# Expert weights fetched as 2 MB of one expert in 16 KB pieces instead of 2 MB of two experts in 8 KB pieces

## The chip, the core and the metric

One core of a Trainium2 chip runs the whole program. The metric is the device time of one execution in microseconds (us); lower is better. TensorE (PE in the profile) multiplies matrices, VectorE (DVE) and ScalarE (ACT) work on tiles, GpSimd (POOL) does little here, SyncE (SP) issues the loads, and 16 DMA engines carry them.

## What is computed

Two layers of a small transformer, float32 throughout, for 256 tokens of width 2048. Each layer is a mixer (layer 0: mLSTM and gated linear attention; layer 1: sparse attention), a layer norm, a mixture of 16 experts, and a layer norm. The change touches the mixture only:

```
# each token picks 2 of 16 experts (comb holds the two gates, 0 elsewhere)
hg = einsum('btd,edf->btef', x, w_gate)      # w_gate[e]: 2048 x 512
hu = einsum('btd,edf->btef', x, w_up)        # w_up[e]:   2048 x 512
h  = silu(hg) * hu * comb
y  = einsum('btef,efd->btd', h, w_down)      # w_down[e]: 512 x 2048
```

All three matrices of all 16 experts of both layers, 403 MB, are read from memory once. Of each, a partition holds 32 KB in one run (`gate_w`, `up_w`, `down_w` are arranged so).

## The kernel before

**Experts in pairs.** The experts of a layer are done two at a time, eight pairs `x` = 0 to 7. Up to 64 tokens (CAP) of each expert are gathered; matmuls of the two experts alternate (`for e in range(2)`), each with 64 columns of weights, writing to halves of the same PSUM bank. Four pairs make a group: in a group's first pair (`i == 0`) TensorE also gathers the tokens of its eight experts (`gather_tile`, 16 tiles of 4 matmuls, lines 841 and 842; DVE line 1626 and ACT line 1187 copy them out of two banks). So pairs 0 and 4 of each layer carry a gather.

**Steps.** The weights of a pair come in 12 steps of 2 MB: steps 0 to 3 are gate, 4 to 7 up, 8 to 11 down. I number a layer's steps through, 0 to 95; pair 4 begins with step 48. There are six slots of 2 MB (`step_slot`: three in `arena2`, three in `ring`); step n lands in slot n modulo 6. SP issues load n (`load_step`, line 485) once `step_used` says that step n - 6 has been used. The six first loads of a layer are issued ahead, during the mixer's end. TensorE waits for `loaded`, does the step's 8 matmuls (16 instructions in the profile, since each float32 matmul is run as two), and adds one to `step_used`.

**Between steps.** In the second and later pairs TensorE adds the last pair's result to the tokens (`add_elder`, `scatter`, lines 850 and 851) after steps 1 and 3, and twice around the transposes (line 899) ahead of step 8. Where tokens are gathered, four tiles come ahead of each of the steps 0 to 3, and each of these steps also waits until the tiles have been copied out (`drained`).

**After the experts.** The loads of the second layer norm's rows and, from layer 0, of the next mixer's weights (line 471, into the ring's slots as steps 9 to 11 are used, and line 507) stand behind the expert loads in SP's order. The mixer's weights come in 2 KB pieces. When the last step is used, ACT and DVE read the result out (lines 1197 and 1630), TensorE scatters it (line 850), and the layer norm follows.

Of the kernel before, what the change touches and what calls it, by code (L numbers as in the profile page):

```python
# [18 lines left out]
BANK = 512  # L19
SLOT = 4096  # L20
# [9 lines left out]
CAP = 64  # L30
# [5 lines left out]
HALF = SLOT // 2  # L36
# [46 lines left out]
def program(nc, a, out):  # L83
    first, drained_by, n = {}, "", 0
# [7 lines left out]
    with ctx:  # L92
# [133 lines left out]
        hT_e, o = carve(arena, o, [4, P])  # L226
# [6 lines left out]
        def xc(k):  # L233

            return xc_lo[:, k, :] if k < KT // 2 else xc_hi[:, k - KT // 2, :]

        aff, k = carve(arena, xc_at, [TT, NE])
        sel, k = carve(arena, k, [TT, NE])
        rank, k = carve(arena, k, [TT, NE])
        cmp, k = carve(arena, k, [TT, NE])  # L240
        cmp2, k = carve(arena, k, [TT, NE])
        pairs6, k = carve(arena, k, [TT * NG, 6])
        gsc, k = carve(arena, k, [TT, NG])
        grank, k = carve(arena, k, [TT, NG])
        gcmp, k = carve(arena, k, [TT, NG])
        gcmp2, k = carve(arena, k, [TT, NG])
        chosen, k = carve(arena, k, [TT, NE])
        csum, k = carve(arena, k, [TT, 1])
        crec, k = carve(arena, k, [TT, 1])
        logits_T, k = carve(arena, k, [SEQ])  # L250
# [21 lines left out]
        w_small1, k = carve(arena2, o, [KT, 80])  # L272
        R, o2 = carve(arena2, o, [IH, SEQ])
        rope_t, k = carve(arena2, o, [4, TT * (IH + 1) * IDH // 8])

        X, k = [[None, None], [None, None]], o
# [6 lines left out]
        rope_q, k = carve(arena2, k, [4, TT * GQ * 16])  # L283

        ps = [ctx.enter_context(nc.psum_tensor(f"ps{i}", [P, BANK], FP32)) for i in range(8)]
# [11 lines left out]
        drained = {"A": sem("drained_by_act"), "D": sem("drained_by_dve")}  # L297
# [53 lines left out]
        for lay in range(2):  # L351
            s = {name: sem(f"{name}_{lay}") for name in (
                "step_used", "silu_ready", "pT_full", "pT_ready", "h_ready", "hT_full", "hT_ready",
                "y_hi_ready", "y_ready", "comb_ready", "pick_ready", "h_hi_ready", "h_lo_ready", "acc_ready")}
# [56 lines left out]
        gate_w = a["moe_w_gate"].rearrange("l e (p k) n -> l e p (k n)", k=KT)  # L411
        up_w = a["moe_w_up"].rearrange("l e (p k) n -> l e p (k n)", k=KT)
        down_w = a["moe_w_down"].rearrange("l e (p j) n -> l e p (j n)", j=4)


        def step_slot(st):

            b = st % 6
            return arena2[:, b * SLOT:(b + 1) * SLOT] if b < 3 else ring[:, (b - 3) * SLOT:(b - 2) * SLOT]

        def group_tiles(g):


            return 0 if isinstance(g, int) and g == 0 else 24 * g - 4

        def gather_at(first, n):


            return n if first or n < 4 else n + 1
# [10 lines left out]
        def _(sp):  # L440
# [33 lines left out]

            def step_source(lay, e, st):

                w = (gate_w, up_w, down_w)[st // 4]
                two = w[lay, e:e + 2] if isinstance(e, int) else w[lay, bass.ds(e, 2)]
                return two.rearrange("e p f -> p e f")[:, :, (st % 4) * HALF:(st % 4 + 1) * HALF]

            def load_step(lay, e, x, st):

                if not (isinstance(x, int) and x == 0 and st < 6):
                    sp.wait_ge(M[lay]["step_used"], STEPS * x + st - 5)
                sp.dma_start(step_slot(st).rearrange("p (e f) -> p e f", e=2), step_source(lay, e, st))\
                  .then_inc(M[lay]["loaded"][st % 6], 16)

            def wait_last_pair(st):
# [117 lines left out]
        def _(pe):  # L606
# [121 lines left out]
            for k in range(KT):  # L728
                for at, lo, hi in ((0, 0, NH), (32, NH, 2 * NH), (64, 8, 8 + RANK)):
                    last = nc.tensor.matmul(tile("gates")[at:at + hi - lo, 0:SEQ], w_small0[:, k, lo:hi], hT[:, k, :],  # L730
                                            start=(k == 0), stop=(k == KT - 1), skip_group_check=True)
# [5 lines left out]
            for i in range(2):  # L737
                drained_before(pe, "decay", i)
                for j in range(2):
                    hd = 2 * i + j  # L740
                    last = nc.tensor.matmul(tile("decay", i)[:, j * SEQ:(j + 1) * SEQ], w2[0:RANK, hd * DK:(hd + 1) * DK],
                                            t3[0:RANK, 0:SEQ], start=True, stop=True)
# [24 lines left out]
            for c in range(3):  # L767
                for hp in range(2):
                    i = 2 * c + hp
                    drained_before(pe, "gstate", i)  # L770
                    for j in range(2):
                        hd = 2 * hp + j
                        last = nc.tensor.matmul(tile("gstate", i)[:, j * DV:(j + 1) * DV], kz[:, (c // 2) * NH + hd, c % 2, :],
                                                V[:, c // 2, NH + hd, 0:DV], start=True, stop=True)
# [9 lines left out]
            for tt in range(TT):  # L784
                pe.wait_ge(state_ready, 6 if tt else 2)
                for hp in range(2):
                    i = 2 * tt + hp
# [19 lines left out]
            def experts(lay):  # L807

                s = M[lay]
# [41 lines left out]
                        nc.tensor.matmul(t, to, y_lo[:, c % 2, :], start=False, stop=True).then_inc(s["full"][tt], 1)  # L851

                def project(x, i, m, bank):
                    st = 4 * bank + m
                    pe.wait_ge(s["loaded"][st % 6], 16 * (2 * x + st // 6 + 1))
                    w = step_slot(st).rearrange("p (e k n) -> p e k n", e=2, k=4)
                    for kk in range(4):
                        k = 4 * m + kk
                        for e in range(2):
                            at = (2 * i + e) * CAP  # L860
                            last = nc.tensor.matmul(ps[bank][e * CAP:(e + 1) * CAP, :], xc(k)[:, at:at + CAP], w[:, e, kk, :],  # L861
                                                    start=(k == 0), stop=(k == KT - 1), skip_group_check=True)
                    last.then_inc(s["step_used"], 1)

                def pair(g, i, first):
                    x = GPAIRS * g + i

                    def add_elder(c):
                        if not (first and i == 0):
                            scatter(x - 1, (i + 1) % 2, c, group_tiles(g) + scatter_at(first, i, c))  # L870

                    for m in range(4):
                        if i == 0:
                            for k in range(4 * m, 4 * m + 4):
                                gather_tile(g, first, k)
                            for b in range(2):
                                pe.wait_ge(s["drained"][b], group_tiles(g) + gather_at(first, 2 * m + 1) + 1)
                        project(x, i, m, 0)
                        if m % 2 == 1:
                            add_elder(m // 2)  # L880
                    project(x, i, 0, 1)
                    project(x, i, 1, 1)

                    pe.wait_ge(s["silu_ready"], x + 1)
                    mine = slice(i * P, (i + 1) * P)
                    for tt in range(TT):
                        nc.tensor.transpose(ps[0][:, tt * P:(tt + 1) * P], pick8[:, tt, mine].bitcast(FP32), ident[:, :])
                    for tt in range(TT):
                        last = nc.tensor.matmul(ps[0][:, SEQ:SEQ + 2], pick8[:, tt, mine].bitcast(FP32), comb_g[:, tt, 2 * i:2 * i + 2],
                                                start=(tt == 0), stop=(tt == TT - 1), skip_group_check=True)  # L890
                    last.then_inc(s["pT_full"], 1)
                    project(x, i, 2, 1)
                    project(x, i, 3, 1)
                    add_elder(2)

                    pe.wait_ge(s["pT_ready"], x + 1)
                    pe.wait_ge(s["h_ready"], x + 1)
                    for j in range(4):
                        last = nc.tensor.transpose(ps[0][:, j * P:(j + 1) * P], h_e[:, j::4], ident[:, :])
                    last.then_inc(s["hT_full"], 1)  # L900
                    add_elder(3)
                    pe.wait_ge(s["hT_ready"], x + 1)
                    if not (first and i == 0):
                        pe.wait_ge(s["y_ready"], 4 * x)
                    for j in range(4):
                        st = 8 + j
                        pe.wait_ge(s["loaded"][st % 6], 16 * (2 * x + 2))
                        w = step_slot(st).rearrange("p (e n) -> p e n", e=2)
                        for c in range(4):
                            for e in range(2):  # L910
                                last = nc.tensor.matmul(ps[2 + c][e * CAP:(e + 1) * CAP, :], hT_e[:, j, e * CAP:(e + 1) * CAP],  # L911
                                                        w[:, e, c * BANK:(c + 1) * BANK], start=(j == 0), stop=(j == 3), skip_group_check=True)
                        last.then_inc(s["step_used"], 1)

                def group(g, first):
                    pe.wait_ge(s["pick_ready"], g + 1)
# [962 lines left out]
```

## Time and profile before

| what | value |
|---|---|
| median of 3 runs | 1990.96 us (1990.54 to 1991.87) |
| the profiled execution, its own time | 1990.97 us |
| its span, first to last instruction | 1988.8 us |
| TensorE busy | 1743.0 us, 88% of the span |
| DVE, ACT busy | 506.9 us, 286.9 us |
| DMA read | 532.67 MB, 269 GB/s over the span |
| expert stretches (about 585 to 1011 us and 1531 to 1957 us) | 421 GB/s |

A busy share is an average over stages with different limits. A row of the timeline gives the start of a group of instructions, how long it took, the engine, the line of the kernel, what it writes and reads, and in brackets how long the engine sat idle before it and what ended that. SPq is SP's queue: its rows are the moments at which loads are issued.

### The profile page before, as it was taken

What the parts mean: (1) busy time and instruction counts of PE and PEld (TensorE: products, weight loads), DVE (VectorE), ACT (ScalarE), POOL (GpSimd) and SP (SyncE); (2) the same over time, 40 slices, a digit from 0 to 9 for tenths busy, and PEclk for the clock granted to TensorE, in tenths of its full rate; (3) what the DMA queues carried; (4) which work ended last, traced back from release to release, by engine and by line L of the source; (5) the groups of instructions that cost most, each with busy time, mean ns of one, the idle gap of its engine ahead of it and who ended that gap; (6) DMA issues with size and microseconds to landing.
All of it is one profiled execution on the core that took longest, in us unless ns stands there. A gap on an engine that the chain in (4) does not pass through costs nothing.

```text
span 1988.8 us, 16588 instructions
## 1 busy us (share of the span) xinstructions
PE 1743.0 (88%) x6849; PEld 869.6 (44%) x6849; DVE 506.9 (25%) x955; ACT 286.9 (14%) x453; POOL 17.7 (1%) x36
## 2 busy tenths in 40 slices
PE   7999999999599888998769999978959978899874
PEld 5884444477343223332234454436834322343221
DVE  1201011445611112111160171324461111211115
ACT  1012011332310001100010001223331000110000
POOL 1000000000000000000000000000000000000000
PEclk9999999999699999999979999989979999999997
DMA  6443433282379999999972433327337999999995
GB/s 226 142 169 127 169 127 127 86 331 90 127 313 421 421 422 421 421 422 421 421 301 85 138 116 127 127 85 268 112 127 302 421 421 421 422 421 421 421 421 214
DMA packets 121327, 535.82 MB, mean 269 GB/s; under 512 B 12916, under 2 KB 12952, under 8 KB 70568
## 3 DMA queue, kind: packets, MB, share of 16 engines
q1 hardware_dynamic: 120680, 530.59, 67.2%
q0 software_dynamic: 576, 4.19, 0.5%
q8 instruction: 55, 0.90, 0.2%
q14 instruction: 16, 0.13, 0.0%
HBM read 532.67 MB, written 2.10 MB: 269 GB/s over the span
## 4 chain that ended last, share of the span: by engine, by line
PE 53%; issue 28%; DMA 13%; DVE 4%; ACT 1%; SPq 1%; POOL 0%; DVEq 0%; POOLq 0%
PE ps L662 22%; DMA ring<-in_moe_w_down 8%; PE ps L861 6%; PE ps L644 6%; DMA ring<-in_moe_w_up 5%; PE ps L686 3%; PE ps L685 3%; PE ps L684 3%; PE ps L911 3%; PE ps L614 1%; PE ps L841 1%; PE ps L1005 1%; PE ps L842 1%; PE ps L970 1%; PE ps L939 0%
## 5 line engine op out<-in xcount | busy, mean ns | idle before, releaser
L662 PE MATMUL ps<-ring,hT 128*128 128x512 f32 x1024 | 441.7, 592 | 0.0
L662 PEld LDWEIGHTS ps<-ring,hT 128*128 128x128 f32 x1024 | 194.0, 190 | 239.9 <-issue 239.6
L911 PE MATMUL ps<-ring,arena 128*64 128x512 f32 x768 | 173.4, 597 | 31.7 <-DMA ring<-in_moe_w_down 31.7
L861 PE MATMUL ps<-arena 128*64 128x512 f32 x768 | 174.5, 598 | 23.6 <-DMA arena<-in_moe_w_up 18.5
L861 PE MATMUL ps<-arena,hT 128*64 128x512 f32 x512 | 115.8, 597 | 28.2 <-DMA arena<-in_moe_w_gate 21.2
L1636 DVE TENSOR_TENSOR arena<-ps,arena 128x512 f32<-128x512 f32 x128 | 82.3, 684 | 203.4 <-PE ps L851 203.4
L861 PE MATMUL ps<-ring,hT 128*64 128x512 f32 x512 | 115.1, 596 | 12.1 <-DMA ring<-in_moe_w_up 12.1
L911 PEld LDWEIGHTS ps<-ring,arena 128*64 128x64 f32 x768 | 51.9, 137 | 151.5 <-issue 89.1
L644 PE MATMUL ps<-hT,ring 128*128 128x256 f32 x512 | 110.8, 379 | 0.0
L1630 DVE TENSOR_TENSOR y_lo<-ps,y_hi 128x512 fp32r<-128x512 f32 x64 | 42.4, 683 | 264.4 <-ACT y_hi L1197 264.4
L861 PEld LDWEIGHTS ps<-arena 128*64 128x64 f32 x768 | 52.0, 136 | 125.4 <-issue 90.2
L684 PE MATMUL ps<-w_lo,x_hi 128*128 128x512 f32 x256 | 101.7, 397 | 4.7 <-DVE x_lo L1839 3.0
L644 PEld LDWEIGHTS ps<-hT,ring 128*128 128x128 f32 x512 | 97.2, 190 | 13.6 <-issue 0.4
L686 PE MATMUL ps<-w_hi,x_lo 128*128 128x512 f32 x256 | 102.2, 399 | 0.0
L685 PE MATMUL ps<-w_hi,x_hi 128*128 128x512 f32 x256 | 101.9, 398 | 0.0
L1489 DVE TENSOR_TENSOR w_lo<-ring,w_hi 128x2048 fp32r<-128x2048 f32 x32 | 73.3, 2293 | 92.9 <-ACT w_hi L1049 92.9
L1197 ACT ACTIVATE y_hi<-ps 128x512 fp32r<-128x512 f32 x64 | 36.5, 596 | 403.1 <-PE ps L911 268.5
L861 PEld LDWEIGHTS ps<-arena,hT 128*64 128x64 f32 x512 | 35.9, 137 | 103.9 <-issue 68.6
L1049 ACT ACTIVATE w_hi<-ring 128x2048 fp32r<-128x2048 f32 x32 | 61.4, 1925 | 109.4 <-PE ps L686 109.4
L861 PEld LDWEIGHTS ps<-ring,hT 128*64 128x64 f32 x512 | 35.8, 137 | 84.5 <-issue 61.5
L861 PE MATMUL ps<-ring,arena 128*64 128x512 f32 x256 | 58.3, 597 | 13.9 <-DMA ring<-in_moe_w_gate 10.6
L850 PE MATMUL ps<-y_hi,pick_T 128*128 128x512 f32 x128 | 59.7, 467 | 10.2 <-DVE arena L1636 7.2
(278 smaller groups left out, 1373.7 us busy)
## 6 DMA issues: line engine op xcount, KB each, us to landing
arena<-in_moe_w_gate SPq DMA_DIRECT2D x48, 2048.0 KB, 24.6
ring<-in_moe_w_down SPq DMA_DIRECT2D x48, 2048.0 KB, 25.8
ring<-in_moe_w_up SPq DMA_DIRECT2D x32, 2048.0 KB, 26.1
arena<-in_moe_w_up SPq DMA_DIRECT2D x32, 2048.0 KB, 24.2
ring<-in_ab_w_in SPq DMA_DIRECT2D x24, 2048.0 KB, 7.9
ring<-in_moe_w_gate SPq DMA_DIRECT2D x16, 2048.0 KB, 25.9
arena<-in_moe_w_down SPq DMA_DIRECT2D x16, 2048.0 KB, 24.1
ring<-in_c_w_in SPq DMA_DIRECT2D x16, 2048.0 KB, 8.2
```

Source lines behind the costliest of these rows:

```text
L644: last = nc.tensor.matmul(tile(stage, j)[:, 0:SEQ], w[:, k, j * P:(j + 1) * P], hT[:, 8 * u + k, :], start=(u + k == 0), stop=(u == 1 and ...
L662: last = nc.tensor.matmul(tile(stage, i)[:, :], hT[:, 8 * u + k, tt * P:(tt + 1) * P], w[:, k, :], start=(u + k == 0), stop=(u == 1 and k ...
L684: nc.tensor.matmul(t, x_h, w_l[:, k, :], start=(part + k == 0), stop=False)
L685: nc.tensor.matmul(t, x_h, w_h[:, k, :], start=False, stop=False)
L686: last = nc.tensor.matmul(t, x_l, w_h[:, k, :], start=False, stop=(part + k == 6))
L850: nc.tensor.matmul(t, to, y_hi[:, c % 2, :], start=True, stop=False)
L861: last = nc.tensor.matmul(ps[bank][e * CAP:(e + 1) * CAP, :], xc(k)[:, at:at + CAP], w[:, e, kk, :], start=(k == 0), stop=(k == KT - 1), s ...
L911: last = nc.tensor.matmul(ps[2 + c][e * CAP:(e + 1) * CAP, :], hT_e[:, j, e * CAP:(e + 1) * CAP], w[:, e, c * BANK:(c + 1) * BANK], start= ...
L1049: act.activation(w_hi[:, q % 2, :], w, ACT.Copy).then_inc(w_hi_ready, 1)
L1489: v.tensor_tensor(lo, w, w_hi[:, q % 2, :].bitcast(FP32), ALU.subtract).then_inc(w_lo_ready, 1)
L1630: v.tensor_tensor(y_lo[:, c % 2, :], ps[2 + c][:, :], y_hi[:, c % 2, :].bitcast(FP32), ALU.subtract).then_inc(s["y_ready"], 1)
L1636: v.tensor_tensor(d, ps[6 + tt][:, :], d, ALU.add).then_inc(s["drained"][tt], 1)
```

## The change

A step is still 2 MB, in the same slot. What lies in it is different: before, it held a quarter of a matrix of both experts (8 KB a partition of each, so two pieces of 8 KB); now, it holds half of a matrix of one expert (one piece of 16 KB a partition). Even steps hold the first expert, odd steps the second. Since each pair of matmuls needs both experts, TensorE now waits for two steps at once, does 16 matmuls on them, and adds two to `step_used` at the end. The order of the matmuls is the same. The gather of tokens moves with it: eight tiles ahead of steps 0 and 1, eight ahead of steps 2 and 3. The scatters and transposes stay where they were in the order.

```
 def step_source(lay, e, st):
-    w = (gate_w, up_w, down_w)[st // 4]
-    two = w[lay, e:e + 2] if isinstance(e, int) else w[lay, bass.ds(e, 2)]
-    return two.rearrange("e p f -> p e f")[:, :, (st % 4) * HALF:(st % 4 + 1) * HALF]
+    w, half, mine = (gate_w, up_w, down_w)[st // 4], st % 4 // 2, st % 2
+    one = w[lay, e + mine] if isinstance(e, int) else w[lay, bass.ds(e + mine, 1)].rearrange("e p f -> (e p) f")
+    return one[:, half * SLOT:(half + 1) * SLOT]
...
-    sp.dma_start(step_slot(st).rearrange("p (e f) -> p e f", e=2), step_source(lay, e, st))\
+    sp.dma_start(step_slot(st), step_source(lay, e, st))\
...
 def project(x, i, m, bank):
-    st = 4 * bank + m
-    pe.wait_ge(s["loaded"][st % 6], 16 * (2 * x + st // 6 + 1))
-    w = step_slot(st).rearrange("p (e k n) -> p e k n", e=2, k=4)
-    for kk in range(4):
-        k = 4 * m + kk
+    st = 4 * bank + 2 * m
+    w = []
+    for e in range(2):
+        pe.wait_ge(s["loaded"][(st + e) % 6], 16 * (2 * x + st // 6 + 1))
+        w.append(step_slot(st + e).rearrange("p (k n) -> p k n", k=8))
+    for kk in range(8):
+        k = 8 * m + kk
         for e in range(2):
...
-    last.then_inc(s["step_used"], 1)
+    last.then_inc(s["step_used"], 2)
...
-    for m in range(4):
+    for m in range(2):
         if i == 0:
-            for k in range(4 * m, 4 * m + 4):
+            for k in range(8 * m, 8 * m + 8):
                 gather_tile(g, first, k)
             for b in range(2):
-                pe.wait_ge(s["drained"][b], group_tiles(g) + gather_at(first, 2 * m + 1) + 1)
+                pe.wait_ge(s["drained"][b], group_tiles(g) + gather_at(first, 4 * m + 3) + 1)
         project(x, i, m, 0)
-        if m % 2 == 1:
-            add_elder(m // 2)
+        add_elder(m)
...
-    for j in range(4):
-        st = 8 + j
-        pe.wait_ge(s["loaded"][st % 6], 16 * (2 * x + 2))
+    for m in range(2):
+        st = 8 + 2 * m
+        w = []
+        for e in range(2):
+            pe.wait_ge(s["loaded"][(st + e) % 6], 16 * (2 * x + 2))
+            w.append(step_slot(st + e).rearrange("p (j n) -> p j n", j=2))
+        for j in range(2 * m, 2 * m + 2):
...
-        last.then_inc(s["step_used"], 1)
+        last.then_inc(s["step_used"], 2)
```

On TensorE, the first use of weights in layer 0, before. Lines 841 and 842 are the gather, line 861 the projection; the names in brackets are the semaphores waited for.

```order
L841 MATMUL ps<-pick,h_hi 128x512
L842 MATMUL ps<-pick,h_lo 128x512
L861 MATMUL ps<-arena,hT 64x512 [waits expert_step_loaded_0_0,tile_drained_0_1,tile_drained_0_0]
L861 MATMUL ps<-arena,hT 64x512 x7
L841 MATMUL ps<-pick,h_hi 128x512 [waits tile_drained_0_0]
L842 MATMUL ps<-pick,h_lo 128x512
L841 MATMUL ps<-pick,h_hi 128x512
L842 MATMUL ps<-pick,h_lo 128x512
```

The same place of the changed kernel, where the projection is line 863.

```order
L841 MATMUL ps<-pick,h_hi 128x512
L842 MATMUL ps<-pick,h_lo 128x512
L863 MATMUL ps<-arena,hT 64x512 [waits expert_step_loaded_0_0,expert_step_loaded_0_1,tile_drained_0_1,tile_drained_0_0]
L863 MATMUL ps<-arena,hT 64x512 x15
L841 MATMUL ps<-pick,h_hi 128x512 [waits tile_drained_0_0]
L842 MATMUL ps<-pick,h_lo 128x512
L841 MATMUL ps<-pick,h_hi 128x512
L842 MATMUL ps<-pick,h_lo 128x512
```

Four more gather tiles stand ahead of it, the wait names two loads, and 16 matmuls follow in one run; the wait for copied tiles comes twice in such a pair of experts instead of four times.

The end of a pair of experts on TensorE, before: steps 10 and 11 (line 911), then steps 0 and 1 of the next pair.

```order
L911 MATMUL ps<-ring,arena 64x512 [waits expert_step_loaded_0_4]
L911 MATMUL ps<-ring,arena 64x512 x7
L911 MATMUL ps<-ring,arena 64x512 [waits expert_step_loaded_0_5]
L911 MATMUL ps<-ring,arena 64x512 x7
L861 MATMUL ps<-arena,hT 64x512 [waits expert_step_loaded_0_0]
L861 MATMUL ps<-arena,hT 64x512 x7
L861 MATMUL ps<-arena,hT 64x512 [waits expert_step_loaded_0_1]
L861 MATMUL ps<-arena,hT 64x512 x7
```

The same place of the changed kernel, the tail of steps 8 and 9 first.

```order
L913 MATMUL ps<-arena 64x512
L913 MATMUL ps<-ring,arena 64x512
L913 MATMUL ps<-ring,arena 64x512 [waits expert_step_loaded_0_5,expert_step_loaded_0_4]
L913 MATMUL ps<-ring,arena 64x512 x15
L863 MATMUL ps<-arena,hT 64x512 [waits expert_step_loaded_0_1,expert_step_loaded_0_0]
L863 MATMUL ps<-arena,hT 64x512 x15
```

Each step's 8 matmuls waited for their own load; now 16 wait for two.

## Rows read from the trace of the kernel before

**Rows 1.** The page: the span, and the DMA engines' share by slice in tenths.

```profile
span 1988.8 us, 16588 instructions
...
DMA  6443433282379999999972433327337999999995
```

**Rows 2.** Windows: busy time of each engine, granted clock, DMA share, GB/s.

```profile
656.00:716.00 60.00, 49.45 (x218) 16.59 (x218) 8.93 (x16) 4.23 (x9) 0.00 (x0) 1.00 1.01 421
1603.00:1663.00 60.00, 49.73 (x222) 16.71 (x220) 8.83 (x16) 3.86 (x7) 0.00 (x0) 1.00 1.01 421
582.40:584.90 2.50, 2.50 (x14) 0.86 (x12) 0.00 (x0) 0.00 (x0) 0.00 (x0) 1.00 1.02 429
1201.00:1204.00 3.00, 3.00 (x9) 1.33 (x8) 0.00 (x0) 0.00 (x0) 0.00 (x0) 1.00 1.05 410
```

**Rows 3.** Timeline of TensorE, pair 2 of layer 0, steps 8 to 11.

```profile
697.84 3.65 PE L911 MATMUL ps<-arena 128*64 128x512 f32 x16
701.41 3.65 PE L911 MATMUL ps<-ring,arena 128*64 128x512 f32 x16
706.38 3.65 PE L911 MATMUL ps<-ring,arena 128*64 128x512 f32 x16 [1.31 <-DMA ring<-in_moe_w_down]
711.35 3.65 PE L911 MATMUL ps<-ring,arena 128*64 128x512 f32 x16 [1.31 <-DMA ring<-in_moe_w_down]
```

**Rows 4.** Layer 0's start: SP's queue, TensorE, and issue to landing (line 485).

```profile
547.65 0.37 SPq L485 DMA_DIRECT2D arena<-in_moe_w_up  x1
...
556.17 0.37 SPq L485 DMA_DIRECT2D arena<-in_moe_w_up  x1
...
573.19 0.37 SPq L485 DMA_DIRECT2D ring<-in_moe_w_down  x1
...
552.49 3.65 PE L861 MATMUL ps<-arena,hT 128*64 128x512 f32 x16 [0.83 <-issue]
...
DMA to landing us min/median/max: 7.3/11.1/14.4
```

**Rows 5.** Layer 0, entry to pair 4: TensorE's timeline, then SP's queue.

```profile
771.06 3.65 PE L911 MATMUL ps<-ring,arena 128*64 128x512 f32 x16 [1.31 <-DMA ring<-in_moe_w_down]
...
788.25 3.65 PE L861 MATMUL ps<-arena,hT 128*64 128x512 f32 x16 [0.83 <-issue]
...
791.93 0.37 SPq L485 DMA_DIRECT2D arena<-in_moe_w_up  x1
...
810.45 0.37 SPq L485 DMA_DIRECT2D ring<-in_moe_w_down  x1
```

**Rows 6.** SP's queue in layer 1, at its start and in pair 4.

```profile
1493.61 8.89 SPq L485 DMA_DIRECT2D arena<-in_moe_w_up  x2
...
1519.16 7.23 SPq L485 DMA_DIRECT2D ring<-in_moe_w_down  x3
...
1756.36 5.09 SPq L485 DMA_DIRECT2D ring<-in_moe_w_down  x2
```

**Rows 7.** Timeline of TensorE at the end of the experts, layers 0 and 1.

```profile
1011.19 3.65 PE L911 MATMUL ps<-ring,arena 128*64 128x512 f32 x16 [1.32 <-DMA ring<-in_moe_w_down]
1016.35 0.49 PE L850 MATMUL ps<-y_hi,pick_T 128*128 128x512 f32 x1 [1.51 <-DVE y_lo L1630]
...
1047.98 9.79 PE L939 MATMUL ps<-hT,arena 128*80 128x256 f32 x32 [5.50 <-issue]
...
1956.95 3.65 PE L911 MATMUL ps<-ring,arena 128*64 128x512 f32 x16 [1.30 <-DMA ring<-in_moe_w_down]
```

**Rows 8.** Two pauses of TensorE (timeline), and windows around them.

```profile
358.55 0.70 PE L792 MATMUL ps<-arena 128*128 128x256 f32 x2 [2.15 <-DVEq L1482]
...
398.99 1.33 PE L614 MATMUL ps<-ident,arena 128*128 128x128 f32 x5 [3.04 <-DVE arena L1451]
...
340.00:370.00 30.00, 27.85 (x106) 15.10 (x106) 13.13 (x26) 10.64 (x25) 1.65 (x1) 1.00 0.29 108
398.00:405.00 7.00, 6.01 (x29) 6.01 (x30) 4.39 (x6) 3.58 (x6) 1.28 (x2) 0.51 1.03 398
```

More of the change, by code:

```diff
@@ L853, in project @@
                 def project(x, i, m, bank):
-                    st = 4 * bank + m
-                    pe.wait_ge(s["loaded"][st % 6], 16 * (2 * x + st // 6 + 1))
-                    w = step_slot(st).rearrange("p (e k n) -> p e k n", e=2, k=4)
-                    for kk in range(4):
-                        k = 4 * m + kk
+                    st = 4 * bank + 2 * m
[5 more added lines that the diff above has]
+                        k = 8 * m + kk
                         for e in range(2):
                             at = (2 * i + e) * CAP
-                            last = nc.tensor.matmul(ps[bank][e * CAP:(e + 1) * CAP, :], xc(k)[:, at:at + CAP], w[:, e, kk, :],
+                            last = nc.tensor.matmul(ps[bank][e * CAP:(e + 1) * CAP, :], xc(k)[:, at:at + CAP], w[e][:, kk, :],
                                                     start=(k == 0), stop=(k == KT - 1), skip_group_check=True)
-                    last.then_inc(s["step_used"], 1)
+                    last.then_inc(s["step_used"], 2)
                 def pair(g, i, first):
@@ L870, in add_elder @@
                             scatter(x - 1, (i + 1) % 2, c, group_tiles(g) + scatter_at(first, i, c))
-                    for m in range(4):
+                    for m in range(2):
                         if i == 0:
-                            for k in range(4 * m, 4 * m + 4):
+                            for k in range(8 * m, 8 * m + 8):
                                 gather_tile(g, first, k)
                             for b in range(2):
-                                pe.wait_ge(s["drained"][b], group_tiles(g) + gather_at(first, 2 * m + 1) + 1)
+                                pe.wait_ge(s["drained"][b], group_tiles(g) + gather_at(first, 4 * m + 3) + 1)
                         project(x, i, m, 0)
-                        if m % 2 == 1:
-                            add_elder(m // 2)
+                        add_elder(m)
                     project(x, i, 0, 1)
-                    project(x, i, 1, 1)
                     pe.wait_ge(s["silu_ready"], x + 1)
@@ L891, in pair @@
                     last.then_inc(s["pT_full"], 1)
-                    project(x, i, 2, 1)
-                    project(x, i, 3, 1)
+                    project(x, i, 1, 1)
                     add_elder(2)
@@ L904, in pair @@
                         pe.wait_ge(s["y_ready"], 4 * x)
-                    for j in range(4):
-                        st = 8 + j
-                        pe.wait_ge(s["loaded"][st % 6], 16 * (2 * x + 2))
[L908 to L912, printed above, removed]
-                        last.then_inc(s["step_used"], 1)
+                    for m in range(2):
[5 more added lines that the diff above has]
+                        for j in range(2 * m, 2 * m + 2):
+                            for c in range(4):
+                                for e in range(2):
+                                    last = nc.tensor.matmul(ps[2 + c][e * CAP:(e + 1) * CAP, :], hT_e[:, j, e * CAP:(e + 1) * CAP],
+                                                            w[e][:, j % 2, c * BANK:(c + 1) * BANK], start=(j == 0), stop=(j == 3), skip_group_check=True)
+                        last.then_inc(s["step_used"], 2)
                 def group(g, first):
```

## The prediction

> **What bounds the kernel now.** I first read the page's slices [rows 1]: the DMA engines are at nine tenths or more in two long stretches and much lower elsewhere. Those stretches are the experts of the two layers. The windows [rows 2] say the same exactly: 421 GB/s at a DMA share of 1.01 in both layers, while TensorE is busy 49 of 60 us. So the 12 steps of a pair of experts take the time of their 24 MB. The timeline [rows 3] shows how: in steady state TensorE starts a step each time a load lands, 4.97 us apart (706.38, 711.35), works for 3.65 us and idles 1.3 us for the next one. Where two steps follow without a pause their starts are 3.57 us apart (697.84, 701.41); I count 3.58 a step. In steady state, then, TensorE's work is hidden, and three things alone move the end: the beat of the loads, any idle time of the DMA engines within a layer, and what TensorE still does after the last load.
>
> **Idle DMA before.** It exists at the start of each layer only. The first six loads have long landed; load 6 waits for step 0, which waits for the gather. SP issues it at 547.65, load 7 at 556.17, load 8 one such interval later and load 9 at 573.19 [rows 4]: 8.5 us apart, more than a load's 4.97. The shortest time from issue to landing is 7.3 us, so an idle DMA engine needs 2.3 us before data flow. The second candidate is pair 4, where TensorE again gathers: there it falls behind, up to the release of step 51 at 810.45 [rows 5]. Load 47 landed about 771.0 (TensorE started on it at 771.06); the eight loads up to 55 follow at 4.97, so the queue is full until 810.8. Load 56 stands behind them, issued with the release of step 50 some 8.5 us before, so at 810.45 there are 5.3 us of queue, over the 2.3 that are needed. This is the narrowest place of the kernel.
>
> **The change, part by part** (for layer 0; layer 1 has the same intervals: issues at 1493.61 and 1519.16, 25.5 us apart as in layer 0, and the release in pair 4 at 1756.36 [rows 6]).
>
> *Start: +3.3 us.* Slots come free in twos. Steps 0 and 1 are released together where step 1 was: 556.17, less one wait for copied tiles that is gone (0.83 us [rows 4]), 555.3. Steps 2 and 3: 573.19 less two such waits, 571.5. Load 8 then lands at 571.5 + 7.3 = 578.8 and load 9 at 583.8; before, load 9 landed at 573.19 + 7.3 = 580.5. The next release comes 7 us after 571.5, while load 9 still runs, so the queue stays full from there.
>
> *Pair 4: +4.2 us.* In steady state TensorE now waits until the second load of two has landed and then works 7.16 us instead of 3.58. It enters pair 4 at about 778.2 instead of 774.65, 3.6 us later. Steps 50 and 51 are released at 810.45 + 3.6 - 2 x 0.83 = 812.4 [rows 5]. Load 56, without which the queue would now be empty, is issued at 812.4 too. So load 55 ends at 771.0 + 8 x 4.94 = 810.5 (the beat is the next part but one), and new data flow at 812.4 + 2.3 = 814.7: the DMA engines idle for 4.2 us. The releases of 48 and 49 (791.93 + 3.6 - 0.83 = 794.7 against a queue until 800.6) and of 52 and 53 (a scatter and two steps, some 8.2 us, after 812.4, against a queue until 824.6) are in time.
>
> *End: +3.6 us.* The last load used to be followed by one step of work [rows 7]; now two steps remain. TensorE goes on to the scatter, layer norm and next mixer from there, so this is on the path in full. The next mixer's weights, queued on SP behind the expert loads, are held back by the same step counts. They are at most 6.9 MB, 17 us at 410 GB/s, and their first use at 1047.98 is 33 us behind the last step's end at 1014.8 [rows 7]; they stay hidden.
>
> *Beat of the loads: -3.3 us.* Pieces cost something each. With one transfer in flight and 2 KB pieces the engines moved 410 GB/s, with 8 KB pieces 429 GB/s [rows 2]. Divided by 16 engines that is 79.9 ns for 2048 bytes and 305.5 ns for 8192: 0.0367 ns a byte and 4.7 ns a piece. A 2 MB load has 16 pieces of 8 KB per engine and will have 8 of 16 KB, which saves 8 x 4.7 = 0.038 us of 4.97. Over the 86 loads from 10 to 95: 3.3 us. Bounds: nothing, if pieces of 16 KB are carried as two of 8; and if the 5.2 ns by which an 8 KB piece of the full stretch (4.97 us / 16 = 310.7 ns) is slower than the lone one is a price of the piece too, another 8 x 5.2 ns, 7.0 us in all. I take the lower of the two prices, since it is the one that the two piece sizes show.
>
> By the Trainium skill, "DMA: Bandwidth & Descriptors", section "Why small descriptors are slow (HBM only)", each packet costs about 3 cycles inside the engine; at the fabric clock that the page gives that is 3.5 ns. The trace's 4.7 ns agrees roughly; the page's figure would make this part 2.4 us instead of 3.3.
>
> *TensorE's clock: +1.5 us.* The granted clock is 1.00 in the expert stretches (2.4 GHz) [rows 2], with pauses of 1.3 us. Now the pause behind two steps with nothing between them (after steps 8 and 9, and after 10 and 11) becomes 9.88 - 7.2 = 2.7 us. A pause of 2.15 us left the clock at 1.00, one of 3.04 us was followed by 0.51 over 7 us, which is the 1.2 GHz level [rows 8]. 2.7 lies between. A fall costs up to half of 7 us, 3.5; in the middle of a layer the next pause takes it up, but at the entry to pair 4 and at the last two steps it counts. Two places at 0 to 3.5 us each; I take 0.75 each.
>
> The Trainium skill, "TensorE: Matmul & The Clock Gate", section "HAM oscillation — how this bites in real kernels", warns of just this pattern, a burst of matmuls and then a wait for a DMA; it speaks against the change, and is the third rival below.
>
> The other edits cost nothing: ACT and DVE wait for even counts of `step_used` (4, 8, 12), which still come at the end of the same steps; the order of matmuls, and with it the alternation of the experts, is the same; SP's issues of the even step now wait for the odd one, with nothing else between them in its queue.
>
> **Sum.** 3.3 + 4.2 + 3.6 - 3.3 + 1.5 = 9.3 us a layer, 18.6 us for two. The profiled execution took 1990.97 us, as the median of the runs (1990.96): 2009.6 us.
>
> **Rivals.**
> 1. *No gain in the beat* (16 KB pieces are carried no faster): 3.3 + 3.9 + 3.6 + 1.5 = 12.3 a layer, 2015.6 us. For it: the trace has no 16 KB load, and most of the 5.2 ns above may be memory, not pieces.
> 2. *The larger gain in the beat, to 4.89 us, and no clock fall*: 3.3 + 4.6 + 3.6 - 7.0 = 4.5 a layer, 2000 us. Should it be larger still, the sign turns: the three losses, about 11.5 us a layer, are paid back by a beat shorter by 11.5 / 86 = 0.13 us, 4.84 us or 433 GB/s. That is above the 429 of the lone 8 KB transfer, so I give it little. It would end at 1985 to 1991 us.
> 3. *The clock falls often*: in many pauses TensorE drops to half speed. Two steps then take up to 10.7 us against a beat of 9.9; lag grows, pair 4 stalls by the full 3.5 us more, the end too, and a little remains in between: 3.3 + 7.7 + 7.1 - 3.3 + 1 = 15.8 a layer, 2022.6 us. Against it: a late TensorE has no pause, so the fall undoes itself.
> 4. *16 KB pieces are slower* than 8 KB ones, so that the beat goes to 5.05 or more: 2025 us and beyond. Nothing in the trace shows it.
>
> **How the numbers follow.** The forecast with its small changes (2003 to 2014) 0.50; rival 1 0.18; rival 2 within 1996 to 2003 0.12; its other end, same or faster, 0.10; rival 3 0.07; rival 4 0.03. The range from 1998 to 2018 leaves out rival 4, most of rival 3 and the turned sign. 0.2% is about 4 us, what a measurement of this kernel can tell from no change. Slower 0.90, same 0.07, faster 0.03.
>
> **What would show it.** In the changed kernel's trace: SP's issues in twos; at the start of each layer two loads at about 555.3 and two at 571.5; an idle stretch of the DMA engines of some 4 us near 811 to 815 and again in layer 1, where before there was none; TensorE's last run of line 913 twice as long, 7.2 us behind the last load; starts of line 863 9.88 us apart in the full stretch with pauses of 2.7 us, and GB/s there of 424 or 425 instead of 421. The prediction is wrong if the beat is under 4.90 or not changed at all, if no DMA idle time shows in pair 4, or if the clock row shows 0.9 or less in the expert stretches.

## The result, and the profile after

The changed kernel takes 1998.62 us (median of 5 runs, 1996.22 to 2000.87) against 1990.54 us for the kernel before beside it: a ratio of 1.0045, 95% interval 1.0034 to 1.0055. It is slower, as forecast, but by 8 to 10 us and not by 18.6. The time lies just inside the range, at its lower end.

The page of the changed kernel: span, the granted clock and the DMA engines by slice, and the packets. [rows 1] has the first two of before; there were 121327 packets.

```profile
span 1998.7 us, 16666 instructions
...
PEclk9999999999699999999978999989979999999997
DMA  6343433282279999999972433327237999999994
GB/s 230 136 169 129 166 126 126 89 332 92 119 318 427 427 429 427 383 428 428 428 268 85 137 116 126 126 84 276 103 126 296 429 428 428 428 384 426 429 428 191
...
DMA packets 96751, 535.82 MB, mean 268 GB/s; under 512 B 12916, under 2 KB 12952, under 8 KB 70568
```

A packet is what the profile counts for one piece. There are 24,576 fewer: the 49,152 pieces of 8 KB have become half as many of 16 KB, carried whole. The full slices show 427 to 429 GB/s, where there were 421, and in each layer one slice shows 383 or 384: an idle stretch. The windows that answer to [rows 2]:

```profile
656.00:716.00 60.00, 50.82 (x232) 20.16 (x230) 8.62 (x15) 3.86 (x7) 0.00 (x0) 0.99 1.01 428
1603.00:1663.00 60.00, 50.69 (x222) 19.80 (x218) 8.62 (x15) 3.86 (x7) 0.00 (x0) 0.97 1.01 428
```

The granted clock, the third number from the end, is no longer 1.00. SP's queue at the start of layer 0, to be held against [rows 4], and in pair 4, against [rows 5]:

```profile
555.05 0.81 SPq L485 DMA_DIRECT2D arena<-in_moe_w_up  x2
571.02 0.33 SPq L485 DMA_DIRECT2D arena<-in_moe_w_down  x1
...
794.37 0.84 SPq L485 DMA_DIRECT2D arena<-in_moe_w_up  x2
811.79 0.33 SPq L485 DMA_DIRECT2D arena<-in_moe_w_down  x1
```

The issues come in twos, at 555.05 and 571.02 (forecast 555.3 and 571.5) and at 794.37 and 811.79 (forecast 794.7 and 812.4). The DMA engines' busy tenths in 40 slices of 805 to 820 us, 0.375 us each:

```profile
DMA  8989895625210000000096659979899599998997
GB/s 350 612 350 437 350 437 219 262 87 218 87 44 0 0 0 0 0 0 0 0 393 131 175 218 481 437 306 524 350 481 524 218 524 481 393 481 350 524 437 306
```

There was no idle time here before. Over 808 to 812.5 us the engines run dry, one after the other; load 56 lands 4.0 us later than its turn (than one beat behind load 55). The timeline of TensorE around a pair's last steps and the end of each layer, against [rows 3] and [rows 7]:

```profile
712.36 7.09 PE L913 MATMUL ps<-ring,arena 128*64 128x512 f32 x32 [2.69 <-DMA ring<-in_moe_w_down]
722.15 8.45 PE L863 MATMUL ps<-arena,hT 128*64 128x512 f32 x32 [2.71 <-DMA arena<-in_moe_w_gate]
...
1011.58 8.78 PE L913 MATMUL ps<-ring,arena 128*64 128x512 f32 x32 [2.68 <-DMA ring<-in_moe_w_down]
1021.86 0.50 PE L850 MATMUL ps<-y_hi,pick_T 128*128 128x512 f32 x1 [1.50 <-DVE y_lo L1632]
...
1963.40 7.09 PE L913 MATMUL ps<-ring,arena 128*64 128x512 f32 x32 [1.20 <-DMA ring<-in_moe_w_down]
```

32 instructions in 7.09 us, then a pause of 2.7 us: two steps start 9.79 us apart, which is a beat of 4.894 us a load where 4.969 were needed. Two of these runs take 8.45 and 8.78 us. In them the clock has fallen to half, as the windows over the last one and over two others of this kind show (0.66, 0.57, 0.57 as means):

```profile
1011.00:1016.00 5.00, 4.42 (x14) 1.71 (x16) 0.00 (x0) 0.00 (x0) 0.00 (x0) 0.66 1.00 404
653.00:657.00 4.00, 3.63 (x10) 1.27 (x12) 0.00 (x0) 0.00 (x0) 0.00 (x0) 0.57 0.99 422
1585.00:1589.00 4.00, 3.60 (x10) 1.27 (x12) 0.00 (x0) 0.00 (x0) 0.00 (x0) 0.57 1.02 434
```

**An account by layer.** The landing of each load and the release of each step are in the trace as semaphore events. The times are in us, counted from the first gather matmul of a layer, from one profiled execution each of the kernel before, the change, and the experiments below (layer 0 / layer 1). The beat is the time between two landings in the full stretch; the fourth column adds up by how much loads 56 to 60, behind the gather of pair 4, land later than one beat behind the load ahead of them:

| kernel | load 9 lands | beat | late loads in pair 4, by | last load lands | last step ends | behind the last load |
|---|---|---|---|---|---|---|
| before | 43.3 / 43.2 | 4.969 | none | 473.8 / 473.6 | 477.6 / 477.4 | 3.72 / 3.72 |
| the change | 47.2 / 45.9 | 4.894 | 4.0 / 4.3 | 473.8 / 474.1 | 482.8 / 481.4 | 8.93 / 7.24 |
| pairs only (e1) | 47.1 / 46.0 | 4.970 | 3.4 / 4.9 | 479.9 / 481.2 | 487.1 / 488.5 | 7.24 / 7.24 |
| one expert, 8 KB (e2) | 47.7 / 46.3 | 4.970 | 4.0 / 3.9 | 480.5 / 480.3 | 487.8 / 487.6 | 7.24 / 7.24 |
| tail fine (e4) | 47.3 / 46.7 | 4.895 | 2.7 / 2.5 | 473.3 / 473.5 | 479.2 / 477.6 | 5.89 / 4.18 |
| gather fine (e5) | 42.7 / 42.7 | 4.895 | 4.2 / 4.2 | 473.4 / 473.2 | 482.3 / 480.5 | 8.93 / 7.24 |
| mixed (e6) | 44.1 / 43.1 | 4.899 | 0.9 / 0.9 | 472.4 / 471.0 | 476.1 / 474.7 | 3.72 / 3.72 |
| clock filled (e7) | 47.1 / 45.7 | 4.895 | 4.1 / 4.1 | 474.2 / 473.7 | 481.4 / 481.0 | 7.24 / 7.24 |
| mixed, lead (e8) | 43.0 / 42.6 | 4.899 | 0.3 / 0.4 | 469.5 / 468.9 | 473.2 / 472.6 | 3.72 / 3.72 |
| lead only (e9) | 43.2 / 43.1 | 4.894 | 2.8 / 4.6 | 470.8 / 471.8 | 479.7 / 480.4 | 8.91 / 8.65 |
| the change again (e10) | 47.2 / 45.7 | 4.895 | 4.1 / 5.7 | 474.1 / 475.7 | 483.0 / 482.9 | 8.93 / 7.24 |

A delay of 1.2 to 1.3 us of one or two loads a layer stands in all of them, the kernel before too, and isn't counted as late. The change's layers end 5.2 and 4.0 us later than before, and 0.7 us more goes elsewhere: 9.9 us, the difference of the two spans.

### The profile page after: what moved, and what is told of

The parts are those of the page before. It is cut to its first block, busy times and chain, and to the rows that moved or that the text cites. A ratio compares the mean times of both kernels' runs of the same rounds, so it can differ in the third digit from the quotient of the medians.

```text
span 1998.7 us, 16666 instructions
## 1 busy us (share of the span) xinstructions
PE 1752.5 (88%) x6849; PEld 905.6 (45%) x6849; DVE 506.5 (25%) x955; ACT 286.6 (14%) x453; POOL 17.7 (1%) x36
## 4 chain that ended last, share of the span: by engine, by line
PE 53%; issue 28%; DMA 13%; DVE 4%; ACT 1%; SPq 1%; POOL 0%; DVEq 0%; POOLq 0%
PE ps L662 22%; DMA ring<-in_moe_w_down 6%; DMA ring<-in_moe_w_up 6%; PE ps L644 6%; PE ps L863 5%; PE ps L913 4%; PE ps L684 3%; PE ps L686 3%; PE ps L685 3%; PE ps L614 1%; PE ps L841 1%; PE ps L1007 1%; PE ps L842 1%; PE ps L972 1%; PE ps L941 1%
## 5 line engine op out<-in xcount | busy, mean ns | idle before, releaser
L863 PE MATMUL ps<-arena 128*64 128x512 f32 x768 | 239.4, 630 | 42.2 <-DMA arena<-in_moe_w_up 24.1
L913 PE MATMUL ps<-ring,arena 128*64 128x512 f32 x768 | 232.3, 610 | 21.0 <-DMA ring<-in_moe_w_down 21.0
L863 PEld LDWEIGHTS ps<-arena 128*64 128x64 f32 x768 | 77.3, 144 | 176.7 <-issue 176.7
L913 PEld LDWEIGHTS ps<-ring,arena 128*64 128x64 f32 x768 | 75.8, 140 | 96.6 <-issue 96.6
L913 PE MATMUL ps<-arena 128*64 128x512 f32 x256 | 115.0, 602 | 1.5 <-ACT arena L1223 1.4
L863 PE MATMUL ps<-ring,arena 128*64 128x512 f32 x256 | 115.0, 603 | 0.0
L863 PEld LDWEIGHTS ps<-arena,hT 128*64 128x64 f32 x512 | 43.4, 141 | 100.0 <-issue 100.0
L863 PEld LDWEIGHTS ps<-ring,hT 128*64 128x64 f32 x512 | 41.2, 137 | 82.5 <-issue 82.5
```

## Experiments

**The schedule without the pieces** (e1). The transfers of before, used and released in twos.

```
 # the changed kernel, with
+    two = w[lay, e:e + 2] if isinstance(e, int) else w[lay, bass.ds(e, 2)]
+    return two.rearrange("e p f -> p e f")[:, :, (st % 4) * HALF:(st % 4 + 1) * HALF]
...
+    w.append(step_slot(st + e).rearrange("p (e k n) -> p e k n", e=2, k=4))
...
+    matmul(..., xc(k)[:, at:at + CAP], w[kk // 4][:, e, kk % 4, :], ...)
```

> The transfers of before (2 MB, two experts, pieces of 8 KB), but waited for, used and released in twos, with the gather in eights, as in the change. Theory P (the piece): the change's shorter beat comes from the pieces of 16 KB; here the beat stays at 4.97 us, 421 GB/s, and the losses of the pairing stand alone: 3.0 (start) + 3.9 (pair 4) + 3.6 (end) + 0 to 2 (clock) a layer, 2011 to 2015 us. Rival S (the schedule): the longer runs of matmuls or the issues in twos are what let the DMA engines run at 428 GB/s; then 428 GB/s here too, and about 1999 us.

Measured: 2012.18 us, ratio 1.0118 (1.0101 to 1.0134). The windows:

```profile
656.00:716.00 60.00, 53.08 (x230) 20.82 (x228) 8.61 (x15) 3.86 (x7) 0.00 (x0) 0.95 1.01 421
1603.00:1663.00 60.00, 51.56 (x222) 20.54 (x220) 8.61 (x15) 3.86 (x7) 0.00 (x0) 0.94 1.01 421
```

421 GB/s, with TensorE in the rhythm of the change. The schedule doesn't make the faster beat, and alone it costs 23 us, as expected. So the change is a loss of 23 us against a gain of some 14 from the larger pieces.

**One expert, pieces of 8 KB** (e2). The change with its 16 KB fetched as two pieces that don't adjoin.

```
-    return one[:, half * SLOT:(half + 1) * SLOT]
+    return one.rearrange("p (a b f) -> p a b f", a=2, b=2)[:, :, half, :]
...
-    sp.dma_start(step_slot(st), step_source(lay, e, st))\
+    sp.dma_start(step_slot(st).rearrange("p (a f) -> p a f", a=2), step_source(lay, e, st))\
```

> The changed kernel, except that each 2 MB of one expert is fetched as two pieces of 8 KB a partition that do not adjoin (the first and third, or second and fourth quarter of the matrix), so the weights meet the wrong rows of the tokens. Theory P (the piece): 421 GB/s, a beat of 4.97 us, and the time of the run with pairs alone, 2011 to 2015 us. Rival L (the place): what was slow before is the alternation between two experts that lie 4 MB apart; then 428 GB/s, 4.89 us, and the time of the change, about 1999 us.

Measured: 2013.0 us, ratio 1.0120 (1.0104 to 1.0137), and in the trace a beat of 4.970 us:

```profile
656.00:716.00 60.00, 50.24 (x224) 19.55 (x222) 8.61 (x15) 3.86 (x7) 0.00 (x0) 0.97 1.01 421
```

It doesn't matter from how many experts a transfer takes its bytes; the size of the piece does.

**The price of a piece** (e3). Loads alone, in seven stages. The block names the stages and is not the kernel's own text.

```
stage(2 KB pieces); stage(4 KB); stage(8 KB, one expert); stage(8 KB, two experts)
stage(16 KB); stage(32 KB, 4 MB a load); stage(8 KB, 1 MB a load)
# load n of a stage is issued when the load that held its slot before has landed
```

> Loads alone, 24 of 2 MB a stage, six in flight, nothing computed; the token rows go to the output unchanged. Stages in order: pieces of 2 KB, 4 KB, 8 KB (one expert), 8 KB (two experts), 16 KB, 32 KB (12 loads of 4 MB, three in flight), and 48 loads of 1 MB with pieces of 8 KB. Theory P: a fixed price a piece, taken from 310.6 ns for 8 KB and 611.8 ns for 16 KB in the full stretches of the two kernels, 9.4 ns and 0.03676 ns a byte: 387, 410, 421, 421, 428, 432 and 421 GB/s. With the price I predicted with (4.7 ns): 410, 419 and so on for the small pieces, and 16 KB no faster than 425. Rival T (the transfer): the price is one of a transfer, not a piece; then the 1 MB stage is slower (415 or less) and the 4 MB stage alone is faster.

Measured, one window in each stage (length, TensorE's clock, DMA share, GB/s):

```profile
50.00:140.00 90.00, 0.00 (x0) 1.00 1.05 387
160.00:260.00 100.00, 0.00 (x0) 1.00 1.03 410
290.00:370.00 80.00, 0.00 (x0) 1.00 1.01 422
400.00:480.00 80.00, 0.00 (x0) 1.00 1.01 422
530.00:620.00 90.00, 0.00 (x0) 1.00 1.01 428
650.00:740.00 90.00, 0.00 (x0) 1.00 1.00 432
770.00:870.00 100.00, 0.00 (x0) 1.00 1.01 422
```

All seven are within 1 GB/s of theory P: 9.4 ns a piece and 0.03676 ns a byte, worked out from 8 and 16 KB alone, give the rates at 2, 4 and 32 KB too, for one expert and two, and for transfers of 1 and 2 MB. In the trace a mean of 6 transfers of 2 MB was in flight with 8 and 16 KB pieces, as planned, but only 3.7 with 2 KB and 4.8 with 4 KB, where SP was 5 us at each issue. The queue was full in each stage even so.

**Fine steps at the end** (e4). Steps 10 and 11 of pairs 3 and 7 in the layout of before. In this and the next ones a function decides which steps have it; SP's loop over the pairs is written out for that, and steps 2m and 2m + 1 hold the same part of the weights in either layout.

```
+def old(i, st):
+    return i == GPAIRS - 1 and st >= 10
...
 def step_source(lay, e, st, i):
+    if old(i, st): (the two-expert source of before)
 def project(x, i, m, bank):
+    if old(i, st): (wait, 8 matmuls, release, twice)
```

> The changed kernel, but steps 10 and 11 of the last pair of each group (pairs 3 and 7) in the layout of before: two experts, 8 KB pieces, each used and released alone. Theory Q (the losses lie where one wait is now for two loads and nothing hides it): the end of each layer comes 3.6 us earlier, and so does the entry to pair 4, whose stall of 4.0 us falls under 1 us; four loads a layer lose 0.075 us each: 1998.6 - 2 x (3.6 + 3.3 - 0.3) = 1985.4 us, faster than before. Rival R (the losses are spread over the stretch as lag or half clock): at most 2 us less than the change, 1996 us or more.

Measured: 1989.97 us, ratio 0.9997 (0.9985 to 1.0008), some 9 us below the change where theory Q had 13. The direction holds, the size doesn't. TensorE's rows ahead of pair 4 tell why:

```profile
750.12 8.78 PE L886 MATMUL ps<-arena 128*64 128x512 f32 x32 [1.99 <-DMA arena<-in_moe_w_up]
...
768.51 7.04 PE L945 MATMUL ps<-ring,arena 128*64 128x512 f32 x32
```

Steps 10 and 11 ran without a pause, 32 instructions in one go: TensorE was already behind when they began, after a run at half clock (8.78 us where 7.1 is the rule) on steps 6 and 7 of this pair. The steps 6 to 9 in twos leave it no slack, since the transposes and two scatters stand among them. The ends of the layers split the two: in layer 0, where the clock fell 18 us before its last two steps, TensorE ends 5.89 us behind the last load; in layer 1, where it had not fallen for 70 us, 4.18; with no loss it is 3.72.

**Fine steps at the gather** (e5). `old` is `i == 0 and st < 4`.

> The changed kernel, but steps 0 to 3 of pairs 0 and 4, those with the gather, in the layout of before: four tiles, one step, one release each. Theory Q (each loss stands at its own place): the start is as before (3.0 us a layer back); in pair 4 TensorE still comes in 3.5 us late, but load 56 is issued one release earlier, so that its stall of 4.0 us falls to 0 to 1.3; the end stays 3.5 us late or later; eight old loads a layer cost 0.6 us. 1998.6 - 2 x (3.0 + 3.4 - 0.6) = 1987.0 us. If the stall in pair 4 stays at 4 us, the late entry and not the release in twos makes it.

Measured: 1999.72 us, ratio 1.0055 (1.004 to 1.007). No gain at all; my expectation of 1987.0 is refuted. The account shows the start of before (load 9 at 42.7), and then load 10 comes 3.4 and 2.0 us late. It waits for step 4, which is released with step 5. In pair 4 the same: loads 57 and 58 are late by 4.2 us together. The idle time had moved, not gone. The DMA share over 815 to 830 us:

```profile
DMA  9898895000000698299979999899799996999989
```

**Fine at the gather, and from step 6 on at the end** (e6). `old` is `(i == GPAIRS - 1 and st >= 6) or (i == 0 and st < 4)`.

> The changed kernel, with steps 0 to 3 of pairs 0 and 4, and steps 6 to 11 of pairs 3 and 7, in the layout of before: fine where TensorE is late or the layer ends, 16 KB pieces elsewhere. Theory Q: none of the three losses is left, and the last six steps before pair 4 and before the end give TensorE time to make up what a half clock has cost. 70 of the loads from 10 to 95 keep the short beat: 1989.1 - 2 x 70 x 0.075 = 1978.6 us. Rival R (something of the loss is in the new layout's stretches themselves): 1983 us or more.

Measured: 1985.53 us, ratio 0.9972 (0.9961 to 0.9983). Faster than before, but not the 1978.6 that was expected; the number is in rival R's range, though the loss lies at the new first release in twos and not spread over the stretch. The end is whole (3.72 us behind the last load), pair 4 loses 0.9, but load 10 is late by 3.3 and 2.0 us as in the run before.

**The clock** (e7). The change, with matmuls on the identity, whose result nobody reads, in TensorE's pauses.

```
+def fill(bank, n):
+    for _ in range(n):
+        for e in range(2):
+            nc.tensor.matmul(ps[bank][e * CAP:(e + 1) * CAP, :], ident[:, e * CAP:(e + 1) * CAP],
+                             hT_e[:, :, :].rearrange("p a b -> p (a b)"), start=True, stop=True, skip_group_check=True)
 # fill(2, 1) ahead of step 6, fill(1, 2) ahead of step 10 and of the next pair's step 0
```

> The changed kernel with idle matmuls, whose result is not used, put where TensorE pauses for two loads with nothing between: one pair of them ahead of step 6, two pairs ahead of step 10 and of the next pair's step 0. Theory K (the pauses of 2.0 to 2.7 us make the clock fall, and what falls near the end or pair 4 is paid): the granted clock stays 1.00 in both expert stretches, the last step ends 7.2 us after the last load in both layers, and the time is 0 to 4 us below the change, 1995 to 1998.6, with less spread between runs. If the clock still falls, the pauses are not what it answers to.

Measured: 1999.67 us, ratio 1.0045 (1.003 to 1.0059). The windows over both stretches, of the change first and then of this run:

```profile
580.00:1010.00 430.00, 377.55 (x1652) 150.87 (x1648) 69.46 (x122) 32.42 (x58) 0.00 (x0) 0.97 1.00 423
1530.00:1963.00 433.00, 379.29 (x1661) 152.02 (x1661) 69.84 (x124) 32.79 (x59) 0.00 (x0) 0.97 1.00 423
```

```profile
580.00:1010.00 430.00, 397.47 (x1790) 157.59 (x1786) 69.47 (x122) 32.40 (x58) 0.00 (x0) 1.00 1.00 423
1530.00:1963.00 433.00, 398.36 (x1802) 158.90 (x1803) 69.89 (x124) 32.78 (x59) 0.00 (x0) 1.00 1.00 423
```

By the trace's record of the granted clock it fell once in the experts of this run, where it fell 15 times in the change's (the last of layer 0 at 1011.6, just behind the window), and both layers end 7.24 us behind the last load. So the pauses make the clock fall. It hardly matters: the time didn't go down (the interval allows 3 us either way) and missed the expected 1995 to 1998.6, and the idle time in pair 4 is the 4.1 us of the change. By the account, which leaves out the stretch between the layers (470.7 us here, the longest of all), the two layers together are 1.8 us shorter than the change's. That is the 1.7 us that a half clock cost at the end of layer 0.

**The lead** (e8). `old` is `(i == GPAIRS - 1 and st >= 6) or (i == 0 and st < 6)`.

> As the mixed run, but the layout of before holds for steps 0 to 5 of pairs 0 and 4, not 0 to 3 (steps 6 to 11 of pairs 3 and 7 as there). Theory L (lead): a release in twos costs one step of the queue's lead wherever TensorE is behind, so the loss only moved to load 10 (2.0 and 3.3 us late) and load 58 (0.9) when steps 0 to 3 were made fine; with two steps more TensorE has caught up. Load 10 comes without delay, load 58 too, and the time is 1985.5 - 2 x (2.6 + 0.7 - 0.3) = 1979.5 us. If the delay moves again, to load 12, by 2 us or more, the lead is not regained by then: 1984 us or more.

Measured: 1980.81 us, ratio 0.9950 (0.9935 to 0.9965): 8 to 10 us faster than the kernel before, 18 us faster than the change. One execution of six took 3725.97 us; there is no profile of it and its cause is unknown. The median of the five others is 1980.35. Load 10 is 1.6 and 0 us late and load 12 is 1.1 and 2.3. These hold the delays of 1.3 us that the kernel before has at load 10 or 13 too, so some 1 us at most is a wait for a slot. In layer 1 load 12 does reach the 2 us named as a sign against the theory, without the time that was to go with it. The end of layer 0:

```profile
1006.21 3.65 PE L945 MATMUL ps<-ring,arena 128*64 128x512 f32 x16 [1.31 <-DMA ring<-in_moe_w_down]
1011.37 0.49 PE L861 MATMUL ps<-y_hi,pick_T 128*128 128x512 f32 x1 [1.51 <-DVE y_lo L1675]
```

One step behind the last load, as in [rows 7], and 5 us earlier.

**The lead alone** (e9). `old` is `i == 0 and st < 6`.

> The changed kernel, with steps 0 to 5 of pairs 0 and 4 in the layout of before, and nothing at the end of the pairs. Theory L: the start is as before, 3.0 us a layer back; in pair 4 the late entry (3.5 us) stays and leaves about 2.4 us of idle DMA in two pieces, at loads 57 and 60, instead of 4.0 at load 56; the end stays 7.2 us or more behind the last load; the older loads cost 0.9 us a layer. 1999 - 2 x (3.0 + 1.6 - 0.9) = 1991.6 us. Theory Q as first put (steps 0 to 3 alone matter) would make it no better than the run with those, 1999.7 us.

Measured: 1996.09 us, ratio 1.0033 (1.0018 to 1.0047). It lies between the two theories' numbers. The start is regained (load 11 at 54.2 and 52.9 where the change has 56.9 and 55.7), as theory L says. In pair 4, 2.8 and 4.6 us are lost instead of 2.4, and both layers end with a run at half clock (8.9 and 8.65 us behind the last load, where I had 7.2 "or more"). The ten runs of this kernel spread over 11 us, as the ten of e4 do; those of the change spread over 5.

**The change again** (e10).

> The changed kernel once more, beside the two above. Theory P and L: beats of 4.894 us, idle DMA of 3.0 to 3.3 us at the start and 4.0 to 4.3 at load 56 in each layer, as in its first profile. Theory K: the places where the clock falls differ from the first profile, and the last step ends either 7.2 or 8.9 us after the last load.

Measured: 1999.41 us, ratio 1.0049 (1.0033 to 1.0065). Beats of 4.895 and 4.894, load 56 late by 4.1 and 5.7 us, the ends 8.93 and 7.24 us behind the last load, and clock falls at other places. The stretch between the two layers' experts, which the change doesn't touch, took 468.8 us in the first profile and 465.4 in this one; over all runs here it took 463.8 to 470.7. A difference of 2 or 3 us between two profiled executions can't be told from that; the account by layer leaves this stretch out.

## Why the prediction was wrong, and where it was right

**In short.** The sign, the three losses and their places were right, the sum was twice too large. What came about is rival 2, the larger gain in the beat (4.5 us a layer, 2000 us), to which I had given 0.12, though with the clock falling, which it had excluded. One of the prediction's own signs of being wrong came true: the beat is 4.894 us, under 4.90. Of 18.6 us forecast the account has 9.2; of the 9.4 between them the beat is 6.3, the start some 1.8 and the clock 1.3.

**Right: the three losses and their places.** The start: issues at 555.05 and 571.02, as forecast within 0.5 us. At load 9 the loss is 3.9 and 2.7 us; by load 12 and 13, past the delay that every kernel has about there, 2.3 and 2.0, and 2.5 and 2.3 without what the shorter beat has given back by then, so 3.3 was too much by some 0.9. Pair 4: 4.0 and 4.3 us, forecast 4.2. The price of restarting an empty queue is right in sum and not in its parts. The last pieces of load 55 end by 809.7, the first of load 56 begin at 812.75, 1.0 us after the issue and not 2.3; but these first ones take 1.0 to 1.4 us where later ones take 0.61, and issue to landing is 7.2 us. The end: 3.5 us without the clock's part, forecast 3.6. The schedule alone, measured in e1, costs 23 us for two layers; the prediction's terms without the beat are 25.2.

**Wrong: the size of the beat's gain.** This is the step that failed: "Beat of the loads: -3.3 us", and in it the sentence that I take the lower of the two prices. The loads land 4.894 us apart instead of 4.969, so 0.075 us a load and 6.4 us over the 86 loads. That is twice the forecast, and 6.3 us too little gain in both layers together. The upper bound named there, 7.0, was near. What I had done was to price a piece from two short windows [rows 2]: 410 GB/s with 2 KB, 429 with 8 KB. I took both for a single transfer in flight. The second was not: SP had issued loads 10 and 11 by 580.1, and load 10 lands at 586.9. But load 7, issued at 556.17 and landed at 563.5 with no other in flight, shows the same rate:

```profile
558.50:562.00 3.50, 2.67 (x13) 1.38 (x13) 1.11 (x2) 0.60 (x1) 0.00 (x0) 1.00 1.01 428
```

With the queue full 2 KB pieces run at 387 GB/s (e3), so 84.7 ns each and not 79.9, and 8 KB pieces take 310.7 and not some 306. Either size costs some 4.7 ns more. The price of a piece is therefore 9.4 ns there, twice what a lone transfer shows, and most of the 5.2 ns that I had set aside as perhaps memory's belongs to the piece. Why a full queue costs more a piece isn't shown. The stretch to be priced is one with a full queue; its own 310.7 ns a piece, and not the 305.5 of a lone transfer, was the row to go by.

The Trainium skill, "DMA: Bandwidth & Descriptors", section "Why small descriptors are slow (HBM only)", has a fixed cost of about 3 cycles a packet inside the engine, 3.5 ns by the page's clock. As the whole price of a piece that is too low here: 9.4 ns with a full queue (e3), 4.7 for a lone transfer; the measurement decides.

**Wrong in size: the clock's price.** Forecast 1.5 us a layer. It did fall, 8 and 7 times, but each fall cost only some 1.7 us of work (a run of 8.78 us where 7.09 is the rule), and the next pause took it up, except at the end of one of the two layers: 0.85 us a layer. The direction "a late TensorE has no pause, so the fall undoes itself" was right; rival 3 did not come about. The row that I leaned on, a pause of 2.15 us that left the clock at 1.00 [rows 8], was one execution's. In the profile of the change the same pause of the same instructions was followed by a fall:

```profile
358.17 0.70 PE L792 MATMUL ps<-arena 128*128 128x256 f32 x2 [2.15 <-DVEq L1484]
...
340.00:370.00 30.00, 27.85 (x104) 14.87 (x103) 13.13 (x26) 11.02 (x26) 1.65 (x1) 0.94 0.29 103
```

So a pause of this length can go either way, and one row could not bound it.

The Trainium skill, "TensorE: Matmul & The Clock Gate", section "HAM oscillation — how this bites in real kernels", has bursts of matmuls and waits for a DMA drop the clock. The traces agree that it drops (15 falls, 1 with the pauses filled), and e7 shows that this costs some 2 us of the time here.

The terms as measured: 2.4 + 4.2 + 3.5 - 6.4 + 0.85 = 4.55 us a layer, and the account gives 5.2 and 4.0, a mean of 4.6.

**What fell on the way.** My theory after the result was that each loss sits at its own place and can be taken out there. e5 refuted it: with the first four steps fine the loss came back at the first release in twos, at full size. What a release in twos costs, by theory L, is one step of the queue's lead (the loads that are issued and have not yet landed), and it is paid at the first moment at which TensorE is behind by more than the queue holds. e6 and e8 differ in the layout of steps 4 and 5 of pairs 0 and 4 alone (and in how a loop of SP that isn't entered is written), and by 4.7 us in their medians, 5.0 in the account. Theory L, formed for that, predicted e8 within 1.3 us and missed e9 by 4.5. In e9 the late entry to pair 4 and the clock at the end both count, and I had the end at its best case; how often it falls so isn't settled by these runs.

**Open.** The delays of 1.2 to 1.3 us that one or two loads a layer have in every kernel. In the kernel before each of them follows an instruction fetch (q8 in the page's queue list, packets of 16 KB that take 1.0 to 1.1 us): loads 10 and 61 of layer 0 and 13 and 64 of layer 1 are the next to land behind the fetches at 584.6, 838.6, 1545.8 and 1799.2 us. In each layer the first of the two is the first fetch after the queue has filled and the second the eighth after that; the seven between them delay no landing. Which DMA engine carries a fetch isn't in the trace, and no experiment was made.

## What to carry to other kernels

Larger pieces and earlier release of buffers pull against each other when the total of buffers stays: count the lead of the queue in transfers at the places where the consumer is slowest, and the work that is left behind the last load. Use the coarse layout where the consumer waits anyhow and the fine one from the first place at which it is behind until it has caught up, and in the last steps (here 8 to 10 us faster than the kernel before, 18 us faster than the coarse layout everywhere). And take the price of a transfer from a stretch in the state that it will be in: a lone transfer shows another one than a full queue.

## What was not expected of the hardware

- With a full queue a DMA piece cost 9.4 ns plus 0.03676 ns a byte, from 2 KB (387 GB/s) to 32 KB (432 GB/s) in e3. A lone transfer showed 4.7 ns a piece (410 GB/s with 2 KB, 428 with 8 KB in the kernel before).
- With pauses of TensorE of 2.0 to 2.7 us between its double steps the granted clock fell to its lower level (1.2 GHz) now and then, 15 times in the experts of the change and once with the pauses filled (e7); with pauses of 1.3 us between single steps it stayed at 1.00 [rows 2, 3]. The same pause of 2.15 us elsewhere was followed by a fall in one execution and by none in another.
- The first pieces behind an empty queue began 1.0 us after the issue and took 1.0 to 1.4 us each instead of 0.61 (16 KB, load 56 of the change).
